# Residual and norm rows fetched inside the last second-table stage, its last four tiles taken chunk by chunk, and residual, square, root and norm done per chunk

## What is computed

```
for i in range(2):
    h = rmsnorm(x, norm1_g[i]) * (1 + scale1) + shift1
    x = x + gate1 * token_mixer(h)          # two kinds of attention, gated and projected
    h = rmsnorm(x, norm2_g[i]) * (1 + scale2) + shift2
    x = x + gate2 * peer_mixer(h)           # per row and head 16 of 16384 experts, tables u and v
return rmsnorm(x, final_g)
```

## Time and profile before

| what | value |
|---|---|
| median of 3 runs | 3883.69 us (3882.17 to 3885.43) |
| the profiled execution: its own time | 3883.39 us |
| the profiled execution: its span | 3881.7 us |
| PE busy | 3505.5 us, 90% of the span |
| DVE busy | 2624.1 us, 68% |
| DMA | 999.71 MB, mean 258 GB/s |
| indirect gathers (q0) | 153600 packets, 553.72 MB |
| DMAs of SP (q1) | 120194 packets, 443.42 MB |

### The profile page before, as it was taken

How to read it: one execution, slowest core, us unless ns; L and a number is a source line. 1 busy time by engine, 2 the same in 40 slices (tenths; PEclk the granted TensorE clock), 3 DMA queues, 4 the chain that set the end, 5 groups by cost and what they waited for, 6 DMA issues and landing times.

```text
span 3881.7 us, 50533 instructions
## 1 busy us (share of the span) xinstructions
PE 3505.5 (90%) x13822; PEld 2245.4 (58%) x13822; DVE 2624.1 (68%) x5585; ACT 981.8 (25%) x2147; POOL 1382.6 (36%) x1220
## 2 busy tenths in 40 slices
PE   4998998999866999999978889989998579999997
PEld 2555444777654448884445554457767544688643
DVE  6555115899899777777555541279999987777774
ACT  1333102323254003330023330123223620133200
POOL 0000001445423665566500000034444245666663
PEclk9999999999988999999989999999998889999999
DMA  6321224788856999999952222168877579999997
GB/s 243 132 103 55 91 83 169 283 314 322 303 171 220 404 394 396 337 386 384 374 198 103 97 82 103 50 251 328 307 273 283 179 295 399 401 381 334 391 390 297
DMA packets 274015, 999.71 MB, mean 258 GB/s; under 512 B 31353, under 2 KB 48249, under 8 KB 262785
## 3 DMA queue, kind: packets, MB, share of 16 engines
q0 software_dynamic: 153600, 553.72, 37.7%
q1 hardware_dynamic: 120194, 443.42, 30.3%
HBM read 971.85 MB, written 25.17 MB: 257 GB/s over the span
## 4 chain that ended last, share of the span: by engine, by line
PE 61%; DVE 24%; issue 5%; DVEq 5%; DMA 3%; ACT 2%; ACTq 0%; POOL 0%; SPq 0%; POOLq 0%
PE ps L605 22%; PE ps L558 12%; PE ps L784 9%; DVE arena L1417 4%; DVE mod L1423 4%; PE ps L548 3%; DVE arena L1207 3%; PE ps L516 2%; DMA arena<-in_u_dram,idx 2%; PE ps L493 2%; PE ps L613 2%; PE ps L637 1%; DVE mod L1437 1%; DVEq L1425 1%; DVE arena L1313 1%
## 5 line engine op out<-in xcount | busy, mean ns | idle before, releaser
L1166 POOL DMA_INDIRECT arena<-in_u_dram,idx x512 | 647.5, 1265 | 1001.4 <-issue 648.4
L558 PE MATMUL ps<-hT,mod 128*128 128x256 f32 x4096 | 927.8, 380 | 0.0
L605 PE MATMUL ps<-arena 128*128 128x512 f32 x2048 | 881.6, 593 | 3.7 <-ACT hT L962 3.7
L1166 POOL DMA_INDIRECT arena<-in_v_dram,idx x512 | 638.8, 1248 | 621.8 <-DVE mod L1423 369.5
L558 PEld LDWEIGHTS ps<-hT,mod 128*128 128x128 f32 x4096 | 760.2, 191 | 93.3
L1417 DVE CUSTOM_DVE_ANT_0 arena<-arena 128x1024 f32<-128x1024 f32 x512 | 616.6, 1223 | 236.7 <-DMA arena<-in_u_dram,idx 233.1
L1423 DVE SCALAR_TENSOR_TENSOR mod<-arena,mod 128x1024 f32<-128x1024 f32 x512 | 657.1, 1283 | 122.7 <-DMA arena<-in_v_dram,idx 93.5
L605 PEld LDWEIGHTS ps<-arena 128*128 128x128 f32 x2048 | 389.6, 190 | 493.3 <-issue 493.2
L978 ACT COPY mod<-ps 128x512 f32<-128x512 f32 x512 | 274.6, 590 | 553.1 <-PE ps L548 553.1
L548 PE MATMUL ps<-const,arena 128*128 128x128 f32 x2048 | 269.0, 275 | 20.1 <-ACT mod L978 19.2
L548 PEld LDWEIGHTS ps<-const,arena 128*128 128x128 f32 x2048 | 239.1, 141 | 51.1 <-ACT mod L978 26.6
(11 more groups left out here) (201 smaller groups left out, 3493.1 us busy)
## 6 DMA issues: line engine op xcount, KB each, us to landing
arena<-in_u_dram SPq DMA_DIRECT2D x256, 512.0 KB, 7.1
arena<-in_v_dram SPq DMA_DIRECT2D x256, 512.0 KB, 6.8
arena<-in_ada_w_dram SPq DMA_DIRECT2D x56, 1024.0 KB, 5.7
arena<-in_w_qkv_dram SPq DMA_DIRECT2D x48, 512.0 KB, 6.3
arena<-in_w_m_dram SPq DMA_DIRECT2D x16, 1536.0 KB, 6.8
arena<-in_w_q_dram SPq DMA_DIRECT2D x32, 576.0 KB, 6.5
gate_scratch<-hT SPq DMA_DIRECT2D x64, 256.0 KB, 2.2
hT<-gate_scratch POOLq DMA_DIRECT2D x128, 128.0 KB, 7.8
```

Of the source, the lines that this page charges most:

```text
L558: last = pe.matmul(ps[:, 6 + tile // 2 % 2, tile % 2 * NT:(tile % 2 + 1) * NT], u_turned[:, tile % 2, k * P:(k + 1) * P], hT[:, k, DT0:SEQ ...
L605: last = pe.matmul(ps[:, 2 * c + n, :], act_t[:, e, c * P:(c + 1) * P], stream[:, slot, n * 512:(n + 1) * 512], start=(half == 0 and e == ...
L1166: pool.indirect_dma_start(out=ring[:, r % RING, :], out_offset=None, in_=table, in_offset=bass.IndirectOffsetOnAxis(ap=idx[:, j % 4, k:k + ...
```

## The change

SP's program: the layer loop is written out instead of being a hardware loop. In the last second-table stage of a layer, `mod`, cos and sin are issued behind v tile 15, and behind v tile 47 the residual (as four DMAs of one chunk) and the next norm's `g_row` (512 KB, spread to all partitions). PE: the last four tiles of that stage are taken with the chunk as the outer loop, and `v_done` counts when chunk 2 is complete. DVE: `add_to_x` counts `x_new` for every chunk of `x`, the two gathered chunks first, then the two of PSUM, each with its own wait. ACT squares a chunk and takes its root when its `x_new` is there. DVE norms chunk by chunk, and clears `bias0` behind all of the norm rows. The end of the kernel goes chunk by chunk too.

```diff
 # SP
-            with sp.Fori(0, DEPTH) as l:
+            load_g(0, 0)
+            for l in range(DEPTH):
                 sp.wait_ge(S["layer_done"], l + 1)
...
-                load_g(l, 0)
                 sp.wait_ge(S["zeros_done"], l + 2)
...
+                    more_v(1, 4)
+                    sp.dma_start(mod[:, SHIFT1:GAIN1 + 1, :], mod_dram[:, :, :]).then_inc(S["x_back"], 16)
+                    sp.dma_start(cos_t, io["cos"]).then_inc(S["x_back"], 16)
+                    sp.dma_start(sin_t, io["sin"]).then_inc(S["x_back"], 16)
+                    more_v(4, 12)
+                    sp.wait_ge(S["topk_done"], UNITS * l + UNITS)
+                    for ch in range(CH):
+                        sp.dma_start(x[:, ch, :], x_dram[:, ch, :]).then_inc(S["x_back"], 16)
+                    if l + 1 < DEPTH:
+                        load_g(l + 1, 0)
+                    else:
+                        sp.wait_ge(S["norm_gain"], 2 * DEPTH + 1)
+                        sp.dma_start(g_row[:, :], io["final_g"].partition_broadcast(P)).then_inc(S["g_in"], 16)
+                    more_v(12, HALF // STREAM)
...
-                sp.wait_ge(S["a_used"], TILES * l + TILES + 2)
-                sp.dma_start(mod[:, SHIFT1:GAIN1 + 1, :], mod_dram[:, :, :]).then_inc(S["x_back"], 16)
-                sp.dma_start(cos_t, io["cos"]).then_inc(S["x_back"], 16)
-                sp.dma_start(sin_t, io["sin"]).then_inc(S["x_back"], 16)
-                sp.wait_ge(S["topk_done"], UNITS * l + UNITS)
-                sp.dma_start(x[:, :, :], x_dram[:, :, :]).then_inc(S["x_back"], 16)
-            sp.wait_ge(S["layer_done"], DEPTH + 1)
-            sp.dma_start(g_row[:, :], io["final_g"].partition_broadcast(P)).then_inc(S["g_in"], 16)
 # PE, value_tiles
-                for e in range(HALF):
+                for e in range(HALF if half == 0 else HALF - STREAM):
...
+                if half == 1:
+                    for c in range(ND):
+                        for e in range(HALF - STREAM, HALF):
+                            slot = e % STREAM
+                            if c == 0:
+                                pe.wait_ge(st_in[slot], 1024 * l + 512 + 16 * (e // STREAM) + 272)
+                            for n in range(2):
+                                last = pe.matmul(ps[:, 2 * c + n, :], act_t[:, e, c * P:(c + 1) * P],
+                                                 stream[:, slot, n * 512:(n + 1) * 512], start=False, stop=(e == HALF - 1))
+                            if c == ND - 1:
+                                last.then_inc(S["st_used"], 1)
+                            elif e == HALF - 1:
+                                last.then_inc(S["v_done"], 1)
 # ACT, norm1 (the end of the kernel in the same way)
                 for ch in range(CH):
+                    act.wait_ge(S["x_new"], CH * l + ch + 1)
                     square_sum(ch)
-                start_root(root0[:, :], ss[:, :], D).then_inc(S["sq_done"], 1)
+                    start_root(root0[:, ch:ch + 1], ss[:, ch:ch + 1], D).then_inc(S["sq_done"], 1)
...
             with act.Fori(0, DEPTH) as l:
-                act.wait_ge(S["layer_done"], l + 1)
 # DVE, add_to_x
                 for c in range(GCH):
                     dve.tensor_tensor(peer_sum[:, c, :], peer_sum[:, c, :], mod[:, GATE2, :], ALU.mult)
-                dve.wait_ge(S["st_used"], TILES * l + TILES + STREAM)
+                dve.drain()
+                for c in range(GCH):
+                    dve.tensor_tensor(x[:, c, :], x[:, c, :], peer_sum[:, c, :], ALU.add).then_inc(S["x_new"], 1)
                 for c in range(ND):
+                    if c == 0:
+                        dve.wait_ge(S["v_done"], l + 1)
+                    else:
+                        dve.wait_ge(S["st_used"], TILES * l + TILES + STREAM)
                     dve.tensor_tensor(h2[:, c, :], ps[:, 2 * c:2 * c + 2, :].rearrange("p a n -> p (a n)"),
                                       mod[:, GATE2, :], ALU.mult)
-                dve.drain()
-                for c in range(GCH):
-                    dve.tensor_tensor(x[:, c, :], x[:, c, :], peer_sum[:, c, :], ALU.add)
-                for c in range(ND):
-                    dve.tensor_tensor(x[:, GCH + c, :], x[:, GCH + c, :], h2[:, c, :], ALU.add)
+                    dve.drain()
+                    dve.tensor_tensor(x[:, GCH + c, :], x[:, GCH + c, :], h2[:, c, :], ALU.add).then_inc(S["x_new"], 1)
 # DVE, the layer loop
             with dve.Fori(0, DEPTH) as l:
+                norm_gain(l, 0)
+                dve.drain()
+                for ch in range(CH):
+                    dve.wait_ge(S["sq_done"], CH * l + ch + 1)
+                    inv_root_mean(rstd[:, ch:ch + 1], root0[:, ch:ch + 1], ss[:, ch:ch + 1], D)
+                    norm_rows(ch, 0, h1)
                 dve.memset(bias0, 0.0).then_inc(S["zeros_done"], 1)
...
-                norm_gain(l, 0)
-                dve.wait_ge(S["sq_done"], l + 1)
-                inv_root_mean(rstd[:, :], root0[:, :], ss[:, :], D)
-                for ch in range(CH):
-                    norm_rows(ch, 0, h1)
 # DVE, the end
-            dve.wait_ge(S["out_sq"], 1)
-            inv_root_mean(rstd[:, :], root0[:, :], ss[:, :], D)
             for ch in range(CH):
+                dve.wait_ge(S["out_sq"], ch + 1)
+                inv_root_mean(rstd[:, ch:ch + 1], root0[:, ch:ch + 1], ss[:, ch:ch + 1], D)
```

More of the change, by code:

```diff
@@ L252, in build @@
             "row_used st_used ut_done ut_ev a_used a_ev iota_mm iota_ev td_done exp_t_done pre_done pt_done pq_ev p_done q_done g_done gm_done gs_done kept_used "
-            "x_out x_back out_sq out_ready out_done "
+            "x_out x_back x_new v_done out_sq out_ready out_done "
             "parked_act parked_dve parked_pool parked_pe parked_sp").split()}
@@ L410, in all_v, with more_v @@
                                              .rearrange("p a (b n) -> p (a b) n", b=2), kept[s]).then_inc(kept_out[s], 16)
[L411 to L416, removed]
+                    def more_v(first, end):
+                        with sp.Fori(first, end) as r:
+                            for s in range(STREAM):
+                                tile = l * TILES + HALF * half + STREAM * r + s
+                                sp.wait_ge(S["st_used"], tile + 1)
+                                park()
+                                load_v(tile, s)
+                    if half == 0:
+                        more_v(1, HALF // STREAM)
+                        return
+                    more_v(1, 4)
[12 more added lines that the diff above has]
+                    more_v(12, HALF // STREAM)
                 load_q(0)
@@ L606, in value_tiles @@
                                              stream[:, slot, n * 512:(n + 1) * 512],
-                                             start=(half == 0 and e == 0), stop=(half == 1 and e == HALF - 1))
+                                             start=(half == 0 and e == 0), stop=False)
                     last.then_inc(S["st_used"], 1)
+                if half == 1:
[11 more added lines that the diff above has]
+                                last.then_inc(S["v_done"], 1)
             def project_v(g, bank, chunks):
@@ L1125, in _ @@
             act.preload_act_table_set("natural_log_exp_and_others")
-            act.wait_ge(S["layer_done"], DEPTH + 1)
             for ch in range(CH):
-                act.activation(h_row[:, :], x[:, ch, :], ACT.Square, accum_out=ss[:, ch:ch + 1])
-                act.drain()
-            start_root(root0[:, :], ss[:, :], D).then_inc(S["out_sq"], 1)
+                act.wait_ge(S["x_new"], CH * DEPTH + ch + 1)
+                square_sum(ch)
+                start_root(root0[:, ch:ch + 1], ss[:, ch:ch + 1], D).then_inc(S["out_sq"], 1)
         @block.gpsimd
@@ L1190, in _ @@
             for name, n in (("layer_done", 1), ("norm_gain", 1), ("dq_ready", 1), ("dk_ready", 1),
-                            ("merged_done", 2), ("row_used", RING), ("gm_done", 2), ("gs_done", 2), ("kept_used", KEPT), ("g_done", G_START)):
+                            ("merged_done", 2), ("row_used", RING), ("gm_done", 2), ("gs_done", 2), ("kept_used", KEPT), ("x_new", CH), ("g_done", G_START)):
                 dve.sem_inc(S[name], n)
@@ L1499, in add_to_x @@
             def add_to_x(l):
-                dve.wait_ge(S["x_back"], 64 * l + 64)
+                dve.wait_ge(S["x_back"], 112 * l + 112)
                 park()
@@ L1504, in add_to_x @@
                     dve.tensor_tensor(peer_sum[:, c, :], peer_sum[:, c, :], mod[:, GATE2, :], ALU.mult)
-                dve.wait_ge(S["st_used"], TILES * l + TILES + STREAM)
-                park()
+                dve.drain()
+                for c in range(GCH):
+                    dve.tensor_tensor(x[:, c, :], x[:, c, :], peer_sum[:, c, :], ALU.add).then_inc(S["x_new"], 1)
                 for c in range(ND):
+                    if c == 0:
+                        dve.wait_ge(S["v_done"], l + 1)
```

(10 more changed lines are left out.)

4 lines of the change are left out of this document (removed).

## The result

| | before | after |
|---|---|---|
| median | 3883.69 us (5 runs, 3882.17 to 3885.43) | 3913.68 us (5 runs, 3906.19 to 3921.23) |
| span of the profiled execution | 3881.7 us | 3911.1 us |
| ratio, with its 95% interval | | 1.0076 [1.0061, 1.009] |
| forecast | | 3911.8 us (3898 to 3919) |

The change makes the kernel 30 us slower, 0.8%. The view that tells it is PE's timeline in the last second-table stage, the answer to the earlier trace rows. Its columns are start, duration, engine, line, and in brackets the idle time ahead and what ended it; each tile is eight records, the last four tiles are those of L624.

The account below looks back on a forecast made before the run. The stage was taken as bound by PE, with no DMA bandwidth idle until the gathers end. Stage waits and clock 29.6, boundary 0.6, start 6.3, end -8.4 sum to +28.1 on 3883.39; median forecast 3911.8 us, range 3898 to 3919.

Parts of the forecast that it names:

- long stretches: From each layer's first mixer product to its last second-table stage: +0.5 us per layer, for DVE's second block.
- Waits in the stage: Last second-table stage: PE waits 3.2 us before v tile 16 and 8.2 before v tile 48, in each layer.
- second wait: PE's wait before v tile 48, behind x and g_row in SP's queue: 8.2 us per layer.
- rate taken: SP's queue when backed up under gathers: 208 GB/s, about half of 409, from an earlier burst.
- fixed part: Part of a v tile's landing time under gathers besides transfer at 208 GB/s: 4.3 us.
- Clock: Lower PE clock after each wait in the stage: 1.7 us lost per wait, bounds nothing and 2.2 us.
- Boundary: From PE's end to the next layer's first mixer product: 31.5 us against 30.9, +0.6 us (bounds -3 and +1.7).
- Start of layer 0: First product at 78.0 us instead of 72.22, held by late weights; +6.3 us with DVE's second block.
- 0.5 us added in each layer for DVE's second block: Mixer start: DVE's second block done 32.1 us after w 0's issue, PE wants it at 31.8; 0.5 us added.
- End: From PE's end to the end of the span: 15.0 us against 23.4, -8.4 us (-7.8 to -9.4).
- Rival B: Last second-table stage: v stream absorbs both loads, SP's queue getting over half the DMA; 3882.2 us, chance 0.13.
- Rival C: Last second-table stage: loads at tile 16 absorbed, those at 48 not; +18.3, 3902 us, chance 0.05.

Follow-up runs that it names:

- e1: Changed kernel with mod, cos and sin issued behind v tile 59, x and g_row behind v tile 63: 3888.87 us, ratio 1.0017.
- e3: Changed kernel with the same mid-stage loads spaced out, at most 512 KB at a time with at least four v tiles between: 3883.04 us, ratio 1.0002.
- e4: Changed kernel with all the loads, 4.19 MB, in one burst behind v tile 47 and none behind v tile 15: 3920.18 us, ratio 1.0099.
- e8: Changed kernel with the four x loads issued from ACT's queue at the same point; other loads stay in SP's queue: 3901.64 us, ratio 1.0044.
- e2: Changed kernel with bias0 cleared at the head of DVE's layer loop instead of behind the norm rows: 3905.65 us, ratio 1.0061.
- e5: Changed kernel with both the spaced-out loads of e3 and the early bias0 memset of e2: 3870.89 us, ratio 0.997.
- e7: As e5, but PE takes the last four v tiles one after the other and chunk 2 waits for the last: 3875.98 us, ratio 0.9981.
- e6: As e5, but DVE refines the roots of three chunks in one set of instructions and one chunk alone: 3864.84 us, ratio 0.9952.

## Why the prediction was right

The forecast of 3911.8 us stands against 3913.68. The mechanism was right in each of its parts, but that the total is so close is in part luck: the stages cost 6.4 us more than forecast, and the long stretches outside of them, forecast at +0.5 us each, came out at -1.8 and -2.5 and hid 5.3 of that. Step by step:

- **Waits in the stage.** Forecast 3.2 and 8.2 us, measured 3.56 and 10.14 in layer 0, 3.51 and 10.07 in layer 1. That it is the queue is shown by e1, e3, e4 and e8 together: not the order of the tiles, not the bytes, but what stands ahead in SP's queue. The mis-sized term is the second wait. The rate taken, 208 GB/s, measured 203 (3.25 MB in 16 us); v tile 48 was there 13.7 + 10.1 = 23.9 us after the reference point, of which 3.670/0.203 = 18.1 are transfer, so the fixed part was 5.8 us and not the 4.3 taken from lone v tiles. It isn't a constant: the first wait leaves 13.7 + 3.6 - 2.621/0.203 = 4.4. Most of the surplus of the second lies near the start of its burst: chunk 1 of x lands 3.7 us behind chunk 0 (3.4 in layer 1), and each piece behind it, up to v tile 48, about 2.5 us after the one before. Why is left open. The stages cost 36.0 us, not 29.6: of the 6.4 us between them 4.5 are in the waits and 1.1 in the clock; 0.8 lie in the seams between the blocks and aren't told apart.
- **Clock.** Forecast 1.7 us for each wait, 6.8 in all. The length of the blocks shows it: 32 tiles take 110.13 us at full clock, 112.97 behind the first wait of layer 0; 12 tiles took 44.19 and 43.56 where three quarters of the 55.10 us of 16 tiles are 41.3. That is 2.8, 2.9, 0 and 2.2 us. Together 7.9, but not 1.7 each. The prediction took every such wait to cost clock; the one of 3.51 us cost none.
- **Boundary.** Forecast 31.5 us, measured 31.4. The turn of DVE's loop was indeed uncovered (3.44 us "issue" ahead of the loop's first instruction; in e2 and e5, where that is the memset, they stand ahead of the memset, 3.62 and 3.53), and the first product waits 7.67 us for weights. e2 takes that wait away and gives the 26.0 us.
- **Start of layer 0.** First product forecast at 78.0, measured 77.92. The bias was taken to land 13.9 us after w 0's issue; DVE was released 13.7 after it, at 84.3, just behind the landing of ada 2 (issued at 73.9, 10.3 us). By the trace, then, the rule of the Trainium skill that a ring is consumed in order holds for the bias (page "DMA: Bandwidth & Descriptors", "Queues, rings and completion order"), and its other half, an earlier completion on few engines, doesn't show. The 0.5 us added in each layer for DVE's second block is there in layer 0 (PE waits 0.56 us for it at 102.3 us) and not in layer 1.
- **End.** Forecast -8.4 us, measured -8.4.
- **What wasn't forecast.** The two long stretches between first product and stage came out 1.8 and 2.5 us shorter. In the eight variants the stretch of layer 0 lies between 1653.9 us (e4) and 1661.4 (e7), with the same program in it, that of layer 1 between 1654.9 (e6) and 1658.6 (e8). The mixer's late start isn't caught up in it: the products that begin at 118.1 us before begin at 124.2 after. So I take this for scatter and no effect; it happened to make up for the larger waits.
- **Rival B** needed 390 GB/s for SP's queue. The trace shows 203, and as many packets for the one queue as for the other. The Trainium skill's rule of turns by packets, in the same section, agrees with equal shares if the turns of both queues carry the same; how long a turn is doesn't show in the trace. **Rival C** (the first burst is absorbed) falls with 3.56 and 3.51 us.

## What to carry to other kernels

A stage in which PE never waits can still have no room in its DMA queue: look at how long a streamed tile may take (buffers times time per tile), how long it takes, and what share the queue gets once it is backed up. A load that is moved into such a stage has to be cut so that each part fits into the difference, with tiles between the parts. Cut in this way 4.2 MB more cost PE 0.35 us at most in a layer in e3 (up to 1.6 in e5 and e6), and in two bursts 36 us in all. Another queue helped, but it took its share from the stream too (a wait of 3.6 us stayed). And when work is moved ahead on one engine, see what counted on the old order: a memset behind the norm rows held back the weights, ate the gain at the boundary and cost 5.7 us at the start; only the end's gain was left.

## What the runs showed that I had not expected

The clock's answer to a wait of PE is not the same each time. Here is a stretch of 2 us behind the first wait of the changed kernel, in layer 0 and in layer 1 (the last three columns are granted clock, DMA share, GB/s):

```profile
1794.00:1796.00 2.00, 2.00 (x4) 0.83 (x3) 1.91 (x3) 1.56 (x3) 0.00 (x0) 0.50 1.02 406
...
3720.00:3722.00 2.00, 2.00 (x6) 0.95 (x5) 1.78 (x8) 0.00 (x0) 0.00 (x0) 1.00 1.03 406
```

The waits were 3.56 and 3.51 us long, at the same place of the same program. After one PE ran at the lower level, 0.50 (1.2 GHz), for some 6 us; after the other at the full 2.4 GHz. In e8 it was the same, 113.04 against 110.14 us for the 32 tiles; in e2 both blocks took 111.83 us, 1.7 more than at full speed. What decides it is left open.

The changed kernel's runs also lie wider apart than before's: 15 us (3906 to 3921) against 3 in the same count of runs (in the first group of experiments 19 runs of the kernel before spread over 10 us, 3878.03 to 3888.06). The granted clock of its five runs goes from 0.956 (3920.65 us) to 0.962 (3906.19 us), in the same order as the times but for one pair. More waits of a length at which the clock may dip or not would do that; it was not tested by itself, and they can't be all of it: e3, whose PE hardly waits in the stage, spreads over 13 us in ten runs (3876.59 to 3889.63).
